# Second attention of a two-block kernel: every odd key tile's product with V as three products of rounded parts, six exponentials in flight, products three key tiles late

## The reference

```
def _attend(q, k, v):            # q (B, 2048, 8, 64); k, v (B, 2304, 2, 64)
    scale = HEAD_DIM ** -0.5
    def one_block(q_blk):        # 128 queries
        s = jnp.einsum('bqhgd,bkhd->bhgqk', q_blk, k).astype(jnp.float32) * scale
        p = jax.nn.softmax(s, axis=-1)
        return jnp.einsum('bhgqk,bkhd->bqhgd', p.astype(v.dtype), v)
```

## Time and profile before

| | |
|---|---|
| median of 3 executions | 5135.75 us (5134.45 to 5138.66) |
| the profiled execution: its time | 5137.85 us |
| the profiled execution: its span, first to last instruction | 5136.0 us |
| TensorE's granted clock, mean over the span | 0.936 of full |
| busy: TensorE, VectorE, ScalarE, GpSimd | 87%, 58%, 38%, 6% |
| stage `attention_2`, first exponential step to last product | about 2595 to 3536 us of the span |
| its granted clock from 2598 us | 1.00 |

### The profile page before, as it was taken

The page is one execution under the profiler, slowest core; times in us unless marked ns, Lnnn a source line. Parts: engine busy times, 40 slices in busy tenths (PEclk is TensorE's granted clock), DMA queues, the critical chain, the costliest instruction groups (busy, mean ns, idle before and its releaser), DMA issues. The chain is left out here.

```text
span 5136.0 us, 58435 instructions
## 1 busy us (share of the span) xinstructions
PE 4449.5 (87%) x20394; PEld 3187.2 (62%) x20394; DVE 2962.7 (58%) x3883; ACT 1940.1 (38%) x3062; POOL 307.9 (6%) x197
## 2 busy tenths in 40 slices
PE   7999699998677988999889999998679199999960
PEld 5777488888564544555455555555467178888750
DVE  6676455554555532333265555554855399999866
ACT  3334233333113421222133333333322177777743
POOL 0000110000000000000000000000000211111122
PEclk9999799999788989999989999999899599999985
DMA  4443400000644233111150000004643188878957
GB/s 166 141 150 137 145 17 25 18 18 32 212 131 154 94 124 120 57 54 56 55 168 13 13 19 13 13 9 123 231 163 125 61 315 319 337 307 335 386 212 286
DMA packets 343973, 687.23 MB, mean 134 GB/s; under 512 B 70304, under 2 KB 226976, under 8 KB 325920
## 3 DMA queue, kind: packets, MB, share of 16 engines
q1 hardware_dynamic: 311072, 595.35, 33.0%
q0 software_dynamic: 14848, 50.36, 2.6%
q10 hardware_dynamic: 17920, 39.85, 2.4%
HBM read 571.39 MB, written 180.93 MB: 146 GB/s over the span
## 5 line engine op out<-in xcount | busy, mean ns | idle before, releaser
L2064 PE MATMUL a_pO<-a_PT,a_V 128*128 128x512 f32 x1152 | 587.7, 592 | 0.0
L2130 DVE TENSOR_REDUCE a_part<-a_pA 128x1 f32<-128x1024 f32 (+1 forms) x384 | 360.8, 953 | 390.3 <-PE a_pA L2031 390.3
L1791 PE MATMUL p_pZ<-p_w_in,p_HT 128*128 128x512 f32 (+1 forms) x1440 | 565.4, 552 | 3.7 <-DMA p_w_in<-in_w_in 3.7
L2100 ACT ACTIVATE a_PT<-a_pB 128x512 f32<-128x512 f32 x576 | 343.9, 597 | 579.5 <-PE a_pB L2054 579.5
L2053 PE MATMUL a_pB<-a_QA,a_KH 128*128 128x512 f32 x576 | 457.9, 795 | 0.7 <-ACT a_QA L2092 0.7
L1791 PEld LDWEIGHTS p_pZ<-p_w_in,p_HT 128*128 128x128 f32 x1440 | 272.1, 191 | 279.3 <-issue 272.8
L951 DVE TENSOR_REDUCE a_maxima<-a_pS 128x1 f32<-128x512 f32 x256 | 176.5, 690 | 177.3 <-PE a_pS L859 176.7
L891 PE MATMUL a_pO<-a_V,a_PT 128*128 128x128 f32 x2048 | 249.5, 275 | 0.3 <-DVE a_PT L964 0.3
L3146 DVE TENSOR_TENSOR e_gate_low<-e_gate_w,e_gate_high 128x4096 fp32r<-128x4096 f32 x48 | 212.1, 4418 | 63.4 <-ACT e_gate_high L3078 63.4
L2031 PE MATMUL a_pA<-a_KH,a_QA 128*128 128x512 f32 (+1 forms) x640 | 203.6, 385 | 50.3 <-DVE a_part L2130 30.5
L891 PEld LDWEIGHTS a_pO<-a_V,a_PT 128*128 128x128 f32 x2048 | 243.5, 192 | 5.6 <-DVE a_PT L964 0.6
(11 more groups left out here) (515 smaller groups left out, 8881.1 us busy)
## 6 DMA issues: line engine op xcount, KB each, us to landing
e_gate_w<-in_moe_w_gate SPq DMA_DIRECT2D x49, 2048.0 KB
e_up_w<-in_moe_w_up SPq DMA_DIRECT2D x48, 2048.0 KB, 12.4
e_down_w<-in_moe_w_down SPq DMA_DIRECT2D x47, 2048.0 KB
between_yb<-e_Y SPq DMA_DIRECT2D x47, 512.0 KB, 7.5
between_x<-m_X SPq DMA_DIRECT2D x32, 512.0 KB, 3.0
r_W<-in_w_ada SPq DMA_DIRECT2D x8, 2048.0 KB, 22.0
between_yb<-a_zeros SPq DMA_DIRECT2D x31, 512.0 KB, 10.8
p_w_in<-in_w_in SPq DMA_DIRECT2D x7, 2048.0 KB, 17.3
```

Source lines behind the costliest of these rows:

```text
L1791: mm = pe.matmul(pZ[n][:, 0:hi - lo], HT[b][:, c, :], w_in[:, c, lo:hi], start=c == 0, stop=c == KC - 1)
L2064: pe.matmul(pO[u % 2][:], V1[:, j, u % HKV, :], PT[:, t % RING, :], start=j == 0, stop=j == KT2 - 1).then_inc(S["o_ps"], 1)
L2100: act.activation(PT[:, t % RING, :], pB[t % 2][:], ACT.Exp, scale=scale).then_inc(S["p_ready"], 1)
L2130: dve.tensor_reduce(part[:, h, r % (NG2 // G4):r % (NG2 // G4) + 1], src, AX_X, ALU.max).then_inc(S["maxed"], 1)
```

## The change

Only `attention_2` is changed. For every odd key tile the exponentials and V are split into a high part, rounded to fp32r, and the rest: PH and PL, VH and VL. The float32 product of that tile becomes three fp32r products, VH with PH, VL with PH and VH with PL (the product of the two low parts is left out). ScalarE makes PH right behind the exponential, VectorE makes PL, always one step later; VH and VL are made once at the start, by ScalarE ahead of the first `row` and by VectorE between the split of the second head's keys and the first unit's steps. Even tiles keep the float32 product. The ring of exponentials has six tiles in place of four, and `apply` stands three steps behind `scores`, not two. VectorE's code is written as one loop over steps, with the other work at the step where TensorE needs it. All else is as it was.

```diff
-    RING = 4
+    RING, LAG = 6, 3
...
+        VH, VL = (k.sb(n, [P, KT2 // 2, HKV, 2 * HD], F32R) for n in ("VH", "VL"))
+        PH, PL = (k.sb(n, [P, RING // 2, QW], F32R) for n in ("PH", "PL"))
...
-                pe.matmul(pO[u % 2][:], V1[:, j, u % HKV, :], PT[:, t % RING, :], start=j == 0, stop=j == KT2 - 1).then_inc(S["o_ps"], 1)
+                g, first, last = u % HKV, j == 0, j == KT2 - 1
+                if t % 2 == 0:
+                    pe.matmul(pO[u % 2][:], V1[:, j, g, :], PT[:, t % RING, :], start=first, stop=last).then_inc(S["o_ps"], 1)
+                    return
+                if t == 1:
+                    pe.wait_ge(S["v_high"], 1)
+                    pe.wait_ge(S["v_low"], 1)
+                n = t // 2
+                pe.wait_ge(S["p_high"], n + 1)
+                pe.matmul(pO[u % 2][:], VH[:, j // 2, g, :], PH[:, n % (RING // 2), :], start=first, stop=False)
+                pe.matmul(pO[u % 2][:], VL[:, j // 2, g, :], PH[:, n % (RING // 2), :], start=False, stop=False)
+                pe.wait_ge(S["p_low"], n + 1)
+                pe.matmul(pO[u % 2][:], VH[:, j // 2, g, :], PL[:, n % (RING // 2), :], start=False, stop=last).then_inc(S["o_ps"], 1)
...
-                if t >= 2:
-                    apply(t - 2)
-            apply(STEPS - 2)
-            apply(STEPS - 1)
+                if t >= LAG:
+                    apply(t - LAG)
+            for t in range(STEPS - LAG, STEPS):
+                apply(t)
...
+            act.wait_ge(S["v_loaded"], 16 * HKV)
+            act.wait_ge(S["v_ones"], 1)
+            act.activation(VH[:], V1[:, 1:KT2:2, :, :], ACT.Copy).then_inc(S["v_high"], 1)
             row(0)
...
                 act.activation(PT[:, t % RING, :], pB[t % 2][:], ACT.Exp, scale=scale).then_inc(S["p_ready"], 1)
+                if t % 2:
+                    act.wait_ge(S["p_ready"], t + 1)
+                    act.activation(PH[:, t // 2 % (RING // 2), :], PT[:, t % RING, :], ACT.Copy).then_inc(S["p_high"], 1)
...
+            def low(t):
+                n = t // 2
+                dve.wait_ge(S["p_high"], n + 1)
+                dve.tensor_tensor(PL[:, n % (RING // 2), :], PT[:, t % RING, :], PH[:, n % (RING // 2), :].bitcast(F32), ALU.subtract).then_inc(S["p_low"], 1)
...
             split_keys(1)
-            for u in range(UNITS):
+            dve.wait_ge(S["v_high"], 1)
+            dve.tensor_tensor(VL[:], V1[:, 1:KT2:2, :, :], VH[:].bitcast(F32), ALU.subtract).then_inc(S["v_low"], 1)
+            for t in range(STEPS):
+                u, j = divmod(t, KT2)
                 i, g = divmod(u, HKV)
-                for r in range(NG2):
-                    if u + 1 < UNITS:
-                        maximum(u + 1, r)
-                    if r == 2 and u >= 1:
-                        finish(u - 1)
-                if u + 1 < UNITS:
+                if j < NG2 and u + 1 < UNITS:
+                    maximum(u + 1, j)
+                if t >= 2 and t % 2 == 0:
+                    low(t - 1)
+                if j == 2 and u >= 1:
+                    finish(u - 1)
+                if j == NG2 and u + 1 < UNITS:
                     top_of(u + 1)
-                if g == 0 and i + 1 < NT:
+                if j == NG2 + 1 and g == 0 and i + 1 < NT:
                     split_queries(i + 1)
+            low(STEPS - 1)
             finish(UNITS - 1)
```

More of the change, by code:

```diff
@@ L1960, in attention_2 @@
         names = """v_loaded v_ones k_zeros k_rows k_split k_high q_zeros q_high q_split max_ps maxed top_ready row_ps row_ready
-            s_ps p_ready o_ps rec_ready o_ready zeros_ready yb_zeroed""".split()
+            v_high v_low p_high p_low s_ps p_ready o_ps rec_ready o_ready zeros_ready yb_zeroed""".split()
         S = {n: k.sem(n) for n in names}
```

## The result

The changed kernel takes **5148.86 us** (median of 15 executions, 5140.13 to 5155.87) against 5135.88 us for the kernel before on the same chip (15 executions, 5133.05 to 5149.14). The ratio is 1.002, with a 95% interval of 1.0012 to 1.0028: slower by 13 us, where 21 us less were forecast. The profiled execution took 5152.52 us, its span is 5150.6 us, its mean granted clock 0.929.

A forecast was written before the change was run, and what follows sets the result against it. TensorE was taken to set the stage's pace. 30 x (-0.68) + 1.0 - 1.4 + 0.2 = -20.6 us from the profiled 5137.85 gave 5117.25; with the median 2.1 lower, 5115 us, range 5097 to 5137.

The forecast's parts named there:

- The gain on TensorE: Products with V in `attention_2`: each odd tile saves 0.19 us as three fp32r products, 1.71 us in a unit.
- the two steps: Odd tiles on TensorE: steps of 1.14 and 1.33 us in turn after j = 12.
- the weight load inside the spacing: TensorE's short products: the 0.19 us load hides within 0.227 us spacing; rival that loads are bare, chance 0.07.
- VectorE's chain: Subtraction between reduction 2 and the reciprocal: reciprocal 0.65 us later, stall grows by 1.03 us to 2.15 in a unit.
- R: Time zero for the stall's chain in a unit: the start of step 2's product for maxima on TensorE.
- second stall: Rival at step 6's product for maxima: VectorE later by 0.7 loses 0.4 us a unit, 5127 us; chance within 0.16.
- ScalarE at nothing: ScalarE's copy of every odd tile's exponential costs nothing: 1.26 us for both, covered by TensorE's steps of 1.33.
- The clock falls: Rival: a 2.1 us stall in each unit could lower TensorE's granted clock, costing tens of microseconds; chance 0.02.
- 30 x (-0.68): Term for the 30 units with a stall: each nets -1.71 + 1.03 = -0.68 us.
- half a stage at half pace: Size guessed for the clock's fall in the attention stage: a loss of tens of microseconds; chance 0.02.
- The start: Stage start, first unit: waits behind V's low part cost 2.7 us once, netting +1.0 us.
- The last two units: Stage end: the last unit has no maxima, only tile 3's subtraction is late by 0.3 us; -1.4 us.

The follow-up runs named there:

- e1: The changed kernel with `finish` moved to steps 12 and 14, reciprocal in two halves, query split in three pieces, so no stall: 5060.79 us, ratio 0.9854.
- e2: The kernel before with `finish` behind the last reduction of the next unit, so no stall, float32 products kept: 5102.80 us, ratio 0.9933.
- e13: e1 with V's low part on GpSimd and every tile as three short products, low parts of even tiles by GpSimd: 5045.89 us, ratio 0.9822.
- e5: The kernel before with only the ring of six and the lag of three, all products float32: 5149.63 us, ratio 1.0027.
- e10: The changed kernel with the subtraction for tile 1 ahead of the 256-column reduction instead of behind it: 5119.82 us, ratio 0.9961.
- e17: e10 with a VectorE multiplication of 32 columns ahead of `finish`, lengthening the idle: 5125.21 us, ratio 0.9977.
- e14: The changed kernel with tile 1's product in float32, ahead of the stall, and a 64-column multiplication ahead of `finish`: 5131.47 us, ratio 0.9989.
- e6: The changed kernel unaltered, run and profiled once more: 5147.32 us, ratio 1.0024 to the kernel before.
- e3: The kernel before with an unused VectorE multiplication of 832 columns ahead of each `finish`, lengthening the stall: 5170.88 us, ratio 1.0067.
- e8: e3 with the second score product left out in seven steps of a unit, shortening the unit: 5144.76 us, ratio 1.0018; total not comparable.
- e9: The changed kernel with the first score product issued twice in seven steps of a unit, lengthening the unit: 5177.09 us, ratio 1.0084.
- e11: The changed kernel with the products of tiles 3 and 5, right behind the stall, in float32 again: 5169.30 us, ratio 1.0064.
- e15: The kernel before with an unused VectorE multiplication of 1344 columns ahead of each `finish`: 5193.01 us, ratio 1.0113, median of two executions.
- e16: e14 with the multiplication ahead of `finish` 136 columns wide instead of 64, lengthening the idle: 5164.41 us, ratio 1.0053.
- e18: e10 with a VectorE multiplication of 112 columns ahead of `finish`, lengthening the idle: 5145.31 us, ratio 1.0014.
- e4: The changed kernel with `finish` ahead of the subtraction in step 2: 5165.68 us, ratio 1.0053.

## Why the prediction was wrong

- **The gain on TensorE was right.** Nine odd tiles at 0.19 us: 1.71 forecast, 1.67 by e1 against e2. The spacing of 0.23, the two steps and the weight load inside the spacing held. The rule of the Trainium skill, TensorE: Matmul & The Clock Gate (Part 3), by which a weight load overlaps only in another row group, is not borne out on 288 tiles: their loads lie inside the spacing.
- **VectorE's chain was right.** Reciprocal at R + 1.38 for 1.42, release at R + 6.64 for 6.68, idle 56.6 us for 57, period 28.91 for 28.9. No second stall, no more table loads.
- **ScalarE at nothing was right** for this change; e13 shows where that ends.
- **The step that failed** is the rival "The clock falls", put at a chance of 0.02 because "it stayed at 1.00 through stalls of 1.1", and with it the term "30 x (-0.68)", which took a stall of 2.15 us to cost its own length. The rows showed the clock at 1.00 behind an idle of 0.86; the change more than doubled that, and nothing in the rows reached so far. The runs show no fall at the 30 stalls of four kernels with an idle of 0.86 to 1.74 (before, e5, e10, e17), nor of e14 with 1.75, and falls in all nine where 1.82 or more stands at all stalls or at every second one (the change, e6, e3, e8, e9, e11, e15, e16, e18); e4, with two idles close together, stands apart. One fall costs 1.6 us, so 14 take back 22 us, and from the first to the last reciprocal the change takes 1.8 us more where the 30 units were to save 20.4. The guess "half a stage at half pace" was wrong in its size too: only about 3.4 us behind a stall run at the lower clock.
- **Small terms.** The start cost 2.9 us for 1.0, since the clock falls there too. The last two units save 0.25 us (50.54 to 50.29) where 1.4 was forecast, but there is a fall in them; without one they would save about 1.8 (48.71 in e10, 48.76 in e17).
- **The stages behind are open.** The falls make up about 24 us of the 34 between 5115 and 5149 us; the rest lies behind the stage, where the prediction had nothing. From the next stage's first DMA to the end of the span the five kernels on the float32 products (before, e2, e3, e5, e15) show 1586.0 to 1590.7 us; thirteen with the short products show 1587.0 to 1604.6, eleven of them 1593.1 or more, e9 and e13 1587.5 and 1587.0. That the code there is the same, and that the DMA of the experts' weights waits somewhat longer in the long ones, is all that is seen. e9 speaks against a simple tie to the change: it computes the same numbers as the change, so the tokens go to the same experts, and doesn't have it. It was not settled.

The falls' number, from 3 to 20 at the same idle, goes with how many stalls lie at the place of the beat where they fall. TensorE: Matmul & The Clock Gate of the Trainium skill (Part 1, What's actually happening) says that the chip judges activity on a beat that runs free of the kernel. The traces agree: the starts of the lower clock keep their distance of 30.72 us through units of different length. By this two things would have to be known before such a change, the idle behind which the clock falls and the length of the unit against the beat; only the first was asked for by the prediction's rival, and the rows of before could give neither. Open is why the stalls at 1.07 to 1.46 us fall in e16 and mostly not in the others.

## What to carry to other kernels

A wait of TensorE has two prices: its length, and, where it is long enough, the lower clock behind it. Where a change makes a stall longer than any that the trace shows at full clock, the second price is unknown and isn't small: here 0.08 us of idle decided over some 20 us. In a loop with a steady period it isn't paid at every stall or at none, but at those that lie badly in time, and they come in runs. Take the stall out first (put the slow operation where nobody waits for its engine): that was worth 33 us alone, and made the same short products worth 42 instead of a loss of 13.

## What had not been expected of the hardware

- TensorE's clock went to its lower level behind idles of 1.82 us on 3 to 20 of 30 occasions, and at these stalls never behind 1.66, 1.74, 1.75 or 1.77. The Trainium skill (TensorE: Matmul & The Clock Gate, Why this matters for your kernels) warns of idle gaps between bursts of products; the rows agree that they cost clock, but the gap that did it here, 1.82 us, is shorter than the one it warns of.
- Two idles close together had falls where one alone of more than the longer of them had none: 1.62 and 0.16 us in e4 (17 falls), 1.35 and 0.28 at the start of the stage in e1, 1.38 and 0.28 there in e17, against 1.66 and 1.74 in e10 and e17. That two such idles count together is a guess from these three.
- The falls keep a beat that the kernel doesn't set, and of the stalls of 1.82 us only those fall that lie at one place of it.
- With GpSimd subtracting beside it (1369 ns for 128x512), VectorE's own subtraction went from 685 to 937 ns on average, and one of 64x2304 from 2.56 to 7.34 us (e13).
